# The order of the expert-row gathers on GpSimd: u and v in turn, or eight u and then eight v

## The reference

```python
q = (xb @ wq).reshape(PEER_BLOCK, PEER_HEADS, 2, PEER_DKEY // 2)
s = jnp.einsum('thpd,pkd->thpk', q, subkeys)
...
top_s, sel = lax.top_k(cand, PEER_TOPK)
idx = jnp.take_along_axis(cidx, sel, axis=-1)
g = jax.nn.softmax(top_s, axis=-1)
u = u_tab[idx]
act = jax.nn.gelu(jnp.einsum('thkd,td->thk', u, xb))
vv = v_tab[idx]
return jnp.einsum('thk,thkd->td', (g * act).astype(vv.dtype), vv)
```

## Time and profile before

| | |
|---|---|
| three runs | 2070.92, 2079.48, 2087.42 us; median 2079.48 |
| profiled execution | 2077.99 us |
| its span from first to last instruction | 2076.0 us |
| U(1,0) issued | 942.68 us |
| U(35,0) issued | 1667.25 us |
| U(48,0) issued | 1948.18 us |
| last gather, V(51,7), issued | 2052.86 us |

### The profile page before, as it was taken

One profiled execution on the slowest core, in us unless ns is written; L12 is line 12 of the kernel. 1 busy time (PEld: TensorE's weight loads), 2 busy tenths in 40 slices (PEclk: granted clock), 3 DMA queues, 4 the chain that ended last, 5 costly groups with the idle time before them and its releaser, 6 DMA issues.

```text
span 2076.0 us, 20836 instructions
## 1 busy us (share of the span) xinstructions
PE 1612.1 (78%) x5461; PEld 763.8 (37%) x5461; DVE 1210.5 (58%) x3129; ACT 475.8 (23%) x1217; POOL 1126.0 (54%) x1168
## 2 busy tenths in 40 slices
PE   6979989992657346777888888698888789699867
PEld 1524546550135012223343334243334344255422
DVE  2222355765668811105766777667766689679873
ACT  1221313130111021212222322223221233232321
POOL 2000011112865644677777767667776777477674
PEclk8989999996865678998999999899999899899989
DMA  8796676773995789999999999999999999799986
GB/s 315 260 350 215 212 264 217 245 246 116 391 360 203 286 348 374 390 415 390 389 419 420 415 371 408 415 338 420 420 405 389 392 404 420 284 417 416 407 328 277
DMA packets 237576, 713.45 MB, mean 344 GB/s; under 512 B 23101, under 2 KB 49055, under 8 KB 237456
## 3 DMA queue, kind: packets, MB, share of 16 engines
q0 software_dynamic: 156672, 570.49, 69.8%
q1 hardware_dynamic: 80488, 140.73, 19.2%
q10 hardware_dynamic: 312, 1.07, 0.2%
HBM read 704.42 MB, written 8.25 MB: 343 GB/s over the span
## 4 chain that ended last, share of the span: by engine, by line
DMA 18%; PE 16%; DVE 11%; issue 8%; POOL 7%; ACT 4%; DVEq 0%; POOLq 0%; ACTq 0%
PE ps_y L2305 10%; DMA v_rows<-in_peer_v_dram,expert_idx_ring 7%; DVE u_rows L2082 6%; DMA v_rows<-in_peer_v_dram,tile_idx 6%; DMA u_rows<-in_peer_u_dram,expert_idx_ring 5%; POOL u_rows L1882 3%; PE ps_r L2279 3%; POOL v_rows L1888 3%; PE ps_y L2320 2%; ACT wt_diag L1974 1%; POOL v_rows L1896 1%; DMA v_rows<-in_peer_v_dram,sample_idx 1%; DVE key_scores_w L2093 1%; DVE top_i L2095 1%; DVE top L2094 1%
## 5 line engine op out<-in xcount | busy, mean ns | idle before, releaser
L2305 PE MATMUL ps_y<-v_rows,wt_diag 128*128 128x512 f32 x1664 | 792.6, 617 | 160.6 <-DMA v_rows<-in_peer_v_dram,expert_idx_ring 71.9
L2305 PEld LDWEIGHTS ps_y<-v_rows,wt_diag 128*128 128x128 f32 x1664 | 307.5, 195 | 584.5 <-issue 555.9
L1882 POOL DMA_INDIRECT u_rows<-in_peer_u_dram,expert_idx_ring x384 | 366.9, 956 | 172.7 <-issue 89.6
L2082 DVE CUSTOM_DVE_ANT_0 u_rows<-u_rows,ps_y 128x1024 f32<-128x1024 f32 x360 | 420.4, 1217 | 65.0 <-DMA u_rows<-in_peer_u_dram,expert_idx_ring 59.7
L1888 POOL DMA_INDIRECT v_rows<-in_peer_v_dram,expert_idx_ring x384 | 364.9, 950 | 120.8 <-issue 97.2
L340 POOL DMA_INDIRECT low_rows<-in_peer_u_dram,tile_idx x128 | 173.0, 1352 | 232.2 <-DVE tile_dots L332 164.9
L606 PE MATMUL ps_z<-w_stream,hT 128*128 128x512 f32 (+5 forms) x560 | 243.9, 592 | 22.6 <-DVE hT L780 17.3
L2320 PE MATMUL ps_y<-v_rows,wt_diag 64*64 64x512 f32 x1024 | 134.7, 644 | 61.6 <-DMA v_rows<-in_peer_v_dram,tile_idx 51.7
L332 DVE CUSTOM_DVE_ANT_0 low_rows<-low_rows,tile_rows 128x1024 f32<-128x1024 f32 x128 | 155.0, 1239 | 42.2 <-DMA low_rows<-in_peer_u_dram,tile_idx 41.8
L1896 POOL DMA_INDIRECT v_rows<-in_peer_v_dram,tile_idx x128 | 121.2, 947 | 77.0 <-PE ps_y L2320 52.5
L606 PEld LDWEIGHTS ps_z<-w_stream,hT 128*128 128x128 f32 (+1 forms) x560 | 99.2, 182 | 145.8 <-issue 113.1
(11 more groups left out here) (433 smaller groups left out, 1601.1 us busy)
## 6 DMA issues: line engine op xcount, KB each, us to landing
w_stream<-in_w_in_dram SPq DMA_DIRECT2D x25, 2048.0 KB, 10.1
w_stream<-in_ada_w_dram SPq DMA_DIRECT2D x12, 2048.0 KB, 12.7
w_stream<-in_peer_wq_dram SPq DMA_DIRECT2D x8, 1024.0 KB, 6.6
wq<-in_peer_wq_dram SPq DMA_DIRECT2D x4, 2048.0 KB, 42.1
w_stream<-in_w_in_dram SPq DMA_DIRECT2D x5, 1568.0 KB, 8.5
w_stream<-in_w_in_dram SPq DMA_DIRECT2D x5, 1536.0 KB, 11.1
u_rows<-in_peer_u_dram,expert_idx_ring POOLq DMA_INDIRECT x384, 7.7
v_rows<-in_peer_v_dram,expert_idx_ring POOLq DMA_INDIRECT x384, 8.4
```

The lines of the kernel that those rows point to most:

```text
L1882: g.indirect_dma_start(u_rows[:, j, :], None, U, bass.IndirectOffsetOnAxis(where[:, j:j + 1], 0))\
L2082: v.tensor_tensor_reduce(u_rows[:, j, :], u_rows[:, j, :], row[:, :], 1.0, 0.0, ALU.mult, ALU.add, dots[:, par, j:j + 1]).then_inc(s["u_us ...
L2305: mm = nc.tensor.matmul(ps_y[:, c * 512:(c + 1) * 512], diag[:, par, j, :], v_rows[:, j, c * 512:(c + 1) * 512], start=(first and j == 0), ...
```

## The change

`step` issues the eight U of its group first, and the eight V of the group in front after them. Nothing else is changed: the same 16 gathers, the same waits, the same buffers, the same code on the other engines.

```diff
                     for j in range(NB):
                         u_gather(i, j, u_where)
+                    for j in range(NB):
                         v_gather(i - 1, j, v_where)
```

## The result

| | before | after |
|---|---|---|
| four runs each | 2070.92 to 2087.42, median 2081.86 us | 2272.60 to 2288.66, median 2280.51 us |
| ratio of after to before, 95% interval | | 1.096 [1.093, 1.100] |
| span of the profiled execution | 2076.0 us | 2278.5 us |
| U(1,0) to U(35,0) | 724.6 us | 830.5 us |
| U(35,0) to U(49,0) | 308.7 us | 400.5 us |

The change makes the kernel 9.6% slower. The predicted time was 2243 us with a range from 2155 to 2325, so the measured median lies inside, 38 us above the forecast. The three stretches of the table grew by 105.9, 91.8 and 4.6 us, together 202.3 of the 202.5 us by which the span grew: all of it lies behind U(1,0).

The account below looks back on a forecast made before the run. GpSimd and the DMA engines, at one pace, bound the kernel; GpSimd's stops are lost. Pairs 70, last tile 86 and end 8 add 164 us to 2077.99, giving 2242, or 2243 as median of three; range 2155 to 2325.

Parts of the forecast that it names:

- 22.3 us from U(s,7) to U(s+1,4): Ring of waits through V landing, sums, scores, keys and dot 4; due after 16.2 us, so GpSimd stops 6.1 us; chance 0.78.
- +70: Slots 0 to 32, 17 pairs of steps: 45.9 us a pair, 780 in all, plus 15 of remaining delays, against 725 before.
- it lands: 6.5 us: Landing of V(s-1,0) in the ring of waits, taken as 6.5 us with bounds 4.4 and 7.7.
- nothing there: Pairs of steps: no loss from TensorE's slower clock, which mostly ends before the next V lands; bound 3.0 us a pair.
- 15 stay: Pairs: of 28 us of other delays, at tile ends and long gather issues, VectorE's new idle time hides about half.
- the stops of 4 to 8 us: Sign: GpSimd idles 4 to 8 us ahead of the fifth U of each even step, 17 times.
- the 365: Sign: the DMA rate in the pairs of steps falls from 420 to about 365 GB/s.
- 86 and 4: Last tile: 86 us more, mainly 12 stops of 7.3 us (88 us); and U(49,0) 4 us later, waiting for dots.
- the burst of sixteen V: End of the kernel: the last sixteen V come in one burst, so TensorE ends 4.4 us later.
- The bytes decide: Rival: GpSimd and DMA engines are full in both orders, stops are made good, no change, 2079 us; chance 0.06.
- The block of u frees the odd steps: Rival: no stop at U(s+1,4), odd stops of 20 us and half of the other 28 go, 2045 us; chance 0.04.
- The clock costs more: Rival: every pair and step pays 3.0 us for TensorE's slower clock, with landings of 7.7, 2366 us; chance 0.12.

Follow-up runs that it names:

- E4: Changed order of gathers, with TensorE making queries and scores ahead of the sums of its slot; 2077.26 us, ratio 0.999 to the kernel before.
- E7: Kernel before, u and v in turn, with queries and scores ahead of the sums; 2067.55 us, ratio 0.995 to the kernel before.
- E1: Changed order of gathers, with VectorE taking the keys behind all eight dots instead of four; 2087.46 us, ratio 1.004 to the kernel before.
- E8: Kernel before, u and v in turn, with the keys behind all eight dots; 2069.17 us, ratio 0.997 to the kernel before.
- E11: Changed order, scores ahead of the sums, ring of indices for eight heads instead of four; 2065.13 us, ratio 0.992 to the kernel before.
- E10: Kernel before, u and v in turn, scores ahead of the sums, index ring of eight heads instead of four; 2051.50 us, ratio 0.985.
- E12: Kernel before, but eight v rows first, then eight u rows, and index ring of eight heads instead of four; 2075.66 us, ratio 0.998.

## Why the prediction was right, and what was mis-sized

**The chain of slot 6.** The prediction counted 22.3 us from U(s,7) to U(s+1,4). In slot 6 of the changed kernel it is 1125.50 - 1101.92 = 23.6. The pieces on TensorE and VectorE:

```profile
1110.87 3.67 PE L2306 MATMUL ps_y<-v_rows,wt_diag 128*128 128x512 f32 x8 [1.53 <-DMA v_rows<-in_peer_v_dram,expert_idx_ring]
...
1119.27 0.30 DVE L2093 MAX8 top<-key_scores 128x8 f32<-128x128 f32 x1 [13.32 <-ACT key_scores L1966]
...
1123.49 1.22 DVE L2083 CUSTOM_DVE_ANT_0 u_rows<-u_rows,ps_y 128x1024 f32<-128x1024 f32 x1
```

Next gather 1.24, landing 1110.87 - 1103.16 = 7.71 (predicted 6.5), sums to MAX8 8.40 (8.33), keys 4.22 (4.22), dot and release 1125.50 - 1123.49 = 2.01 (2.0). Due was 16.2, and the stop is 7.4. VectorE's wait of 13.32 us for the scores is the foretold 13. Every step of the chain is there with its length, but for the landing.

**The pairs: +105.9 for +70.** Two terms of the sum were too small. The first is the step "it lands: 6.5 us". Over the 17 slots with keys it is 8.07 us on average from the issue of V(s,0) to the first sum, above the upper bound of 7.7: 6.6 to 8.2 in twelve, 8.9 to 9.6 in four, and 14.5 in slot 32. Not all of this is landing. In slots 0, 12 and 28 the v rows land within 6.4 us (V(s,3) to V(s,6), whose landing the trace has), but TensorE is still busy with the head's queries, in slot 12 until 1254.4, 9.1 us after V(12,0) was issued; in slot 18 its wait ends with the weights that ScalarE writes. These four make 8 us of the 27, a wait for TensorE that the chain of the prediction did not have; the landing in the other thirteen makes 19. The second is "nothing there" for TensorE's clock: from sums to MAX8 it is 8.1 to 8.4 in thirteen slots, but 10.5, 10.1, 11.0 and 10.9 in slots 2, 16, 18 and 32, on average 8.90 instead of 8.33. 17 x (8.07 - 6.5) + 17 x (8.90 - 8.33) = 36 us, which is the whole miss of the pairs. The "15 stay" of the other delays came out, since 830.5 less 17 pairs of 39.8 + 8.19 leaves 14.7, but by luck and not by the step given for it. Of the 28 us that were to be halved, 11.6 were stops of this same ring: in the kernel before GpSimd already stands still at U(2,4), U(14,4), U(20,4), U(30,4) and U(34,4), for 1.1 to 4.0 us, so in five pairs of 17 the ring had no room. The new stops contain these; nearly all of the other 16 us stayed. Of the signs that the prediction named, the stops of 4 to 8 us came in twelve slots and are longer in the other five (8.8 to 16.7), and the rate in the pairs fell to 348 GB/s, below the 365.

Slot 32, the first of a new tile, shows both. Timelines of SyncE's transfers, GpSimd, TensorE and VectorE there:

```profile
1714.91 0.32 SPq L1843 DMA_DIRECT2D norm_scale<-mod_rows  x1
...
1726.84 0.94 POOL L1888 DMA_INDIRECT v_rows<-in_peer_v_dram,expert_idx_ring  x1 [0.30 <-PE ps_y L2306]
...
1741.34 6.15 PE L2306 MATMUL ps_y<-v_rows,wt_diag 128*128 128x512 f32 x8 [7.67 <-DMA v_rows<-in_peer_v_dram,expert_idx_ring]
...
1752.22 0.29 DVE L2093 MAX8 top<-key_scores 128x8 f32<-128x128 f32 x1 [16.44 <-ACT key_scores L1966]
...
1758.44 0.95 POOL L1882 DMA_INDIRECT u_rows<-in_peer_u_dram,expert_idx_ring  x1 [16.97 <-DVE dots L2083]
```

SyncE issues 18 transfers for the sample's norm from 1714.55 to 1720.35, 16 of them of line 1843 like the first row. V(32,0) then takes 14.5 us to the first sum. TensorE starts its sums behind a gap of 7.67 us, at a granted clock of 0.59 from 1741.3 to 1747.5, so mostly at the lower level of 1.2 GHz, and takes 6.15 us instead of 3.60; GpSimd idles 16.97 us ahead of U(34,4). Before, late landings at the same place cost less, since V stood ahead of the u rows that wait. The landings of line 1888 in the kernel before, 1640 to 1667:

```profile
DMA to landing us min/median/max: 11.1/11.2/14.3
```

They were nearly as late, and most of it was hidden: GpSimd's timeline of the kernel before shows 3.50 us of idling ahead of the same U(34,4) instead of 16.97.

```profile
1654.94 0.94 POOL L1882 DMA_INDIRECT u_rows<-in_peer_u_dram,expert_idx_ring  x1 [3.50 <-DVE dots L2082]
```

The prediction reckoned with the median landing of an undisturbed stretch in a place where, after the change, every landing lies on the path.

The chain that ended last in the changed kernel says the same in another view (start, length, what):

```profile
1667.28 10.80 PE ps_y L2306 x20
1680.24 6.77 DMA v_rows<-in_peer_v_dram,expert_idx_ring
...
1713.50 13.29 PE ps_y L2306 x24
1726.84 14.36 DMA v_rows<-in_peer_v_dram,expert_idx_ring
```

The landing of V stands in it for these pairs: 6.77 us in slot 30, and 14.36 in slot 32.

**The last tile: +91.8 for 86 and 4.** Stops come to 6.97 us on average where 7.3 was predicted, by partly other pieces. The timeline of slot 36, TensorE and VectorE:

```profile
1843.08 6.48 PE L2306 MATMUL ps_y<-v_rows,wt_diag 128*128 128x512 f32 x8 [6.25 <-DMA v_rows<-in_peer_v_dram,expert_idx_ring]
...
1854.11 0.29 DVE L2093 MAX8 top<-key_scores 128x8 f32<-128x128 f32 x1 [7.88 <-ACT key_scores L1966]
...
1857.79 1.21 DVE L2083 CUSTOM_DVE_ANT_0 u_rows<-u_rows,ps_y 128x1024 f32<-128x1024 f32 x1
```

TensorE idles 6.25 us, as foretold, and the stretch from 1843 to 1849 has a granted clock of 0.52, so near 1.2 GHz; from sums to MAX8 it takes 11.03 us, a loss of 2.7. It is 10.6 to 11.0 in ten of the twelve slots and 10.4 on average, so that the loss is 2.05 for the 2 that I took. From the issue of V(s,0) to the first sum it was 6.5 on average for 5.7; keys and release took 0.5 us less each (here 3.68 to dot 4, and 0.28 from its end to 1859.28), which makes up for it. That 91.8 lies so near to the 90 is in part luck. The twelve stops lack 4.4 us (83.6 for 88), and the ring's stop grew by 0.5 and not by 2. On the other side U(49,0) came 8.0 us later beyond the pace than before (16.22 us idle for 8.23) where 4 were put, and other delays of 3.4 us are there where none were to stay.

**The end: +4.6** where the burst of sixteen V was put at 4.4; the 4 for U(49,0) lie in the 91.8.

**The rivals.** "The bytes decide" would have left 2079; with DMA shares of 0.89 and 0.81 the stops are not made good. "The block of u frees the odd steps": it does, step 9 has the bare 19.9 us, but the even steps take far more. "The clock costs more" put it at 2366; it was half right, in four pairs and in the last tile. By the two averages from sums to MAX8 the clock's part in the ring is 17 x 0.57 + 12 x 2.05 = 34 us of the 202.

**Still open.** The residue of 0.4 to 0.7% with the ring cut or loosened (E4 against E7, E1 against E8, E11 against E10). The stops of GpSimd beyond the pace show where it lies. They sum to 69.8 us in E4 and 54.4 in E7, 50.9 in E11 and 42.0 in E10, 73.0 in E1 and 59.5 in E8. In E4 and E11 the fifth u rows still stop for 33.4 and 35.3 us, in E7 and E10 not at all (0.2 us), while there the first u rows and the v rows stop for longer; in E1 nearly all of the difference to E8 lies at U(41,0) and U(49,0). What lengthens these stops is open. In the kernels with blocks of eight or four and no stops at every fifth U (E1 to E4, E11, E12), the mean granted clock over the span of the profiled execution is 0.880 to 0.887, in those in turn 0.902 to 0.918. In E4 the eight sums ahead of U(8,4) took 16.92 us where eight at 1.80 are 14.4, with a granted clock of 0.65 and 0.66 from 1065 to 1075. So TensorE's clock is a near reason, but that is only argued, since no run changed the clock alone. Nor was it tried to load the rows of the next tile at another place.

## What to carry to other kernels

On an engine that takes its instructions in order, the order of its transfers is a schedule: put a transfer on which a long chain hangs ahead of those that wait for the end of that chain. Count the ring once around, issue to landing to sums to scores to keys to dot to the next issue, against the number of issues in between times the pace; what it lacks is lost in every turn, although bytes and busy times stay the same. For the landing take the disturbed stretches too, not the median, as soon as the change puts it on the path; and if a ring costs too much, look at each of its ends: here the keys behind all dots cut it, and the scores ahead of the sums loosened it. Fastest was the order in turn with the scores first and a longer ring of indices.

## What the runs showed of the hardware

A gather of 512 KB lands in 6.5 us (median of line 1888 in the changed kernel), in 7.7 us in the kernel before and in 10.1 in E10, where GpSimd stops least; at one issue per 1.24 us that is eight gathers in flight instead of five. It takes 14.3 to 14.4 us behind SyncE's 18 transfers at the end of a tile. The landings from 1725 to 1737 of the changed kernel:

```profile
DMA to landing us min/median/max: 14.3/14.3/14.4
```

and two slices of 4 us there by busy time:

```profile
1722.00:1726.00 4.00, 4.00 (x11) 1.80 (x10) 2.21 (x5) 1.41 (x6) 3.09 (x4) 1.00 1.03 306
1726.00:1730.00 4.00, 4.00 (x10) 1.71 (x9) 0.00 (x0) 1.24 (x5) 3.08 (x4) 1.00 1.04 302
```

The DMA engines are busy throughout (1.03 and 1.04) and move 302 to 306 GB/s instead of 420. The view of the DMA queues tells where their time goes (packets, MB, share of the 16 engines' time), first from 1722 to 1730 in the changed kernel, then from 1500 to 1520 in the kernel before:

```profile
q0 software_dynamic: 588, 2.14, 89.0%
q1 hardware_dynamic: 128, 0.29, 14.7%
...
q0 software_dynamic: 2307, 8.40, 102.6%
```

The first queue is that of the gathers, the second that of SyncE's transfers. The latter take 14.7% of the time; and a packet of the gathers takes longer beside them, 0.890 x 16 x 8 us / 588 = 194 ns against 1.026 x 16 x 20 us / 2307 = 142 ns. Why it does is not shown. The prediction took the landing from the length of the queue of gathers alone.
